# Head norm of the layer 0 memory queries: from a stage of its own into the tiles of the output gate's projection

## The reference, cut to what matters

```python
def rmsnorm(x, g):
    y = xf * lax.rsqrt(jnp.mean(xf * xf, axis=-1, keepdims=True) + EPS)
    return (y * g)

# mem_attn(pm, mkv, g_q)
q = rmsnorm(pm.reshape(b, s, MEM_HEADS, HEAD_DIM), g_q)
sc = einsum('bshd,bmhd->bhsm', q, mkv[:, :, 0]) * HEAD_DIM ** -0.5
p = softmax(sc)
o = einsum('bhsm,bmhd->bshd', p, mkv[:, :, 1])

# mlstm_mixer: o is the output gate's projection, h the normed mLSTM output
return sigmoid(o) * h
# run_trunk
x = x + concatenate([mix, mem_o]) @ w_out[l]
```

## Time and profile before

| what | value |
|---|---|
| median of 3 runs | 3421.77 us (3414.11 to 3422.32) |
| the profiled execution's own time | 3419.85 us |
| its span, first to last instruction | 3418.1 us |
| mean granted TensorE clock | 0.937 of 2.4 GHz |
| PE, DVE, ACT busy | 91%, 37%, 29% of the span |

### The profile page before, as it was taken

How to read it: one execution, slowest core, us unless ns; L and a number is a source line. 1 busy time by engine, 2 the same in 40 slices (tenths; PEclk the granted TensorE clock), 3 DMA queues, 4 the chain that set the end, 5 groups by cost and what they waited for, 6 DMA issues and landing times.

```text
span 3418.1 us, 49546 instructions
## 1 busy us (share of the span) xinstructions
PE 3093.7 (91%) x20055; PEld 2893.8 (85%) x20055; DVE 1262.7 (37%) x1969; ACT 980.7 (29%) x1658; POOL 344.3 (10%) x342
## 2 busy tenths in 40 slices
PE   6997958899999999998789689888689999999998
PEld 5997928799999999997679467777369999999998
DVE  5112751533322323341031477776143332332331
ACT  4212412423211111130431666655032321111110
POOL 0000130001000101000000234443000010000010
PEclk9998969899999999998799789999789999999999
DMA  4110042011111111112210000000411111111113
GB/s 149 58 44 13 1 131 73 32 37 47 45 50 43 47 47 48 40 52 77 90 59 29 3 1 1 2 1 23 127 75 44 43 43 50 44 48 50 45 43 123
DMA packets 63143, 169.11 MB, mean 49 GB/s; under 512 B 7334, under 2 KB 27923, under 8 KB 61859
## 3 DMA queue, kind: packets, MB, share of 16 engines
q1 hardware_dynamic: 50204, 151.00, 13.6%
q10 hardware_dynamic: 12776, 15.85, 1.4%
HBM read 153.02 MB, written 17.99 MB: 50 GB/s over the span
## 4 chain that ended last, share of the span: by engine, by line
PE 69%; DVE 6%; issue 4%; ACT 3%; DVEq 2%; SPq 2%; DMA 1%; POOL 0%; POOLq 0%; ACTq 0%
PE ps L347 57%; PE ps L2297 1%; PE ps L2254 1%; PE ps L2241 1%; PE ps L1789 1%; PE ps L1382 1%; PE ps L2243 1%; PE ps L1146 1%; PE ps L508 1%; SPq L1761 1%; SPq L1760 1%; DVE jf L2408 0%; PE ps L1349 0%; DVEq L2163 0%; PE ps L1375 0%
## 5 line engine op out<-in xcount | busy, mean ns | idle before, releaser
L347 PE MATMUL ps<-h_hi,w_hi 128*128 128x344 f32 x3360 | 725.0, 325 | 50.0 <-DVE h_lo L406 11.8
L347 PE MATMUL ps<-h_lo,w_hi 128*128 128x344 f32 x3360 | 718.5, 322 | 0.0
L347 PE MATMUL ps<-h_hi,w_lo 128*128 128x344 f32 x3360 | 714.9, 321 | 0.0
L347 PEld LDWEIGHTS ps<-h_hi,w_hi 128*128 128x128 f32 x3360 | 572.4, 190 | 56.0 <-issue 44.2
L347 PEld LDWEIGHTS ps<-h_lo,w_hi 128*128 128x128 f32 x3360 | 574.5, 191 | 0.0
L347 PEld LDWEIGHTS ps<-h_hi,w_lo 128*128 128x128 f32 x3360 | 565.1, 189 | 0.0
L299 DVE TENSOR_TENSOR w_lo<-w_raw,w_hi 128x1024 fp32r<-128x1024 f32 (+1 forms) x202 | 303.4, 1502 | 296.9 <-ACT w_hi L293 296.8
L293 ACT ACTIVATE w_hi<-w_raw 128x1024 fp32r<-128x1024 f32 (+1 forms) x202 | 208.6, 1034 | 520.5 <-PE ps L347 454.3
L1582 POOL TENSOR_TENSOR f_silu<-f_silu,nb_r 128x1032 f32<-128x1032 f32 x44 | 107.3, 2439 | 1758.1 <-ACT f_silu L1546 1758.1
L1504 DVE TENSOR_TENSOR xT<-xT,ps 128x1032 f32 (+1 forms) x64 | 78.7, 1229 | 448.3 <-PE ps L347 448.3
L347 PE MATMUL ps<-hid_hi,w_hi 128*128 128x344 f32 x1056 | 224.0, 320 | 0.0
(11 more groups left out here) (494 smaller groups left out, 3720.6 us busy)
## 6 DMA issues: line engine op xcount, KB each, us to landing
w_raw<-w_gu SPq DMA_DIRECT2D x88, 512.0 KB, 3.5
w_raw<-w_dn SPq DMA_DIRECT2D x32, 448.0 KB, 3.3
w_raw<-w_a SPq DMA_DIRECT2D x27, 512.0 KB, 3.5
w_raw<-w_o SPq DMA_DIRECT2D x16, 512.0 KB, 3.5
w_raw<-w_dn SPq DMA_DIRECT2D x16, 512.0 KB, 3.5
pages<-cmp SPq DMA_DIRECT2D x64, 128.0 KB, 2.5
w_raw<-w_b SPq DMA_DIRECT2D x9, 512.0 KB, 3.5
xT<-xT SPq DMA_DIRECT2D x1, 4128.0 KB, 17.0
```

The lines of the kernel that those rows point to most:

```text
L347: mm = pe.matmul(ps[:, 3 * slot + c, 0:cut], w[:, slot, k * P:(k + 1) * P], a[:, k, c * cut:(c + 1) * cut], start=(k == 0 and w is w_hi an ...
```

## The change

In the segment `a_o` each of the three engines gets a hook. After tile 0 ACT squares both query tiles. After tiles 1 to 4 PE does the six sum matmuls in banks 6 and 7 (two, one, two, one), and ACT takes the Ln of them; after tile 4 ACT also does both Exps, and DVE both multiplications. The stage between fence 6 and fence 7 goes, with its fence, and the later fences are renumbered (18 becomes 17). The order of the other work, SP's included, stays.

```diff
-            seg_act(act, "a_o", evac, first=True, chain=False)
+            seg_act(act, "a_o", evac, first=True, chain=False, hook=lambda i: hq_act(act, i))
...
-            seg_dve(dve, "a_o", evac, first=True, chain=False)
+            seg_dve(dve, "a_o", evac, first=True, chain=False, hook=lambda i: hq_dve(dve, i))
+        hq_p, hq_l = sem("hq_p"), sem("hq_l")
+        def hq_cuts(t, part):
+            lo, hi = ((0, 2), (2, 3))[part]
+            return hq_rt[:, t, lo * CH:hi * CH].rearrange("p (c t) -> p c t", c=hi - lo), ps[:, 6:6 + hi - lo, 0:CH]
+        def hq_act(act, i):
+            b = hn_base["act"]
+            if i == 0:
+                for t in range(2):
+                    act.activation(hq_sq[:, t, :], mix[:, 6 + t, :], ACT.Square).then_inc(hn_sq, 1)
+            elif i < 5:
+                act.wait_ge(hq_p, i)
+                out, sums = hq_cuts((i - 1) // 2, (i - 1) % 2)
+                act.activation(out, sums, ACT.Ln, bias=eps_c[:, 0:1], scale=1.0 / HD).then_inc(hq_l, 1)
+            if i == 4:
+                act.drain()
+                for t in range(2):
+                    act.activation(hq_rt[:, t, :], hq_rt[:, t, :], ACT.Exp, scale=-0.5).then_inc(hn_rt, 1)
+                hn_base["act"] += 2
+        def hq_pe(pe, i):
+            if not 1 <= i < 5:
+                return
+            t, part = (i - 1) // 2, (i - 1) % 2
+            pe.wait_ge(hn_sq, hn_base["pe"] + t + 1)
+            if i > 1:
+                pe.wait_ge(hq_l, i - 1)
+            for c in ((0, 1), (2,))[part]:
+                mm = pe.matmul(ps[:, 6 + c % 2, 0:CH], C("pairs"), hq_sq[:, t, c * CH:(c + 1) * CH], start=True,
+                               stop=True)
+            mm.then_inc(hq_p, 1)
+            if part == 1:
+                pe.sem_inc(hn_ss, 1)
...
+        def hq_dve(dve, i):
+            if i == 4:
+                hnorm_dve(dve, lambda t: mix[:, 6 + t, :], lambda t: mix[:, 6 + t, :], 2, N,
+                          lambda t: G("g_mem_q", 0), hq_rt)
...
             ogate_act(act)
             fence(act, 6)
-            hnorm_act(act, lambda t: mix[:, 6 + t, :], 2, CH, 3, hq_sq, hq_rt)
+            attend_act(act, 0)
             fence(act, 7)
-            attend_act(act, 0)
-            fence(act, 8)
...
-            seg_pe(pe, "a_o")
+            seg_pe(pe, "a_o", hook=lambda i: hq_pe(pe, i))
             fence(pe, 6)
-            hnorm_pe(pe, 2, CH, 3, hq_sq)
+            attend_pe(pe, 0)
             fence(pe, 7)
-            attend_pe(pe, 0)
-            fence(pe, 8)
```

More of the change, by code:

```diff
@@ L2464, in nsa_pool @@
             pool.memset(ckB[64:80, :, :].bitcast(F32), 0.0)
-            pool.wait_ge(fence_s, 3 * 14)
+            pool.wait_ge(fence_s, 3 * 13)
             Q_pool(pool, 0, 0)
@@ L2779, in _ @@
             load_seg(sp, "kv")
-            sp.wait_ge(fence_s, 3 * 9)
+            sp.wait_ge(fence_s, 3 * 8)
             bias_sp(sp)
@@ L2783, in _ @@
             load_seg(sp, "b_q")
-            sp.wait_ge(fence_s, 3 * 13)
+            sp.wait_ge(fence_s, 3 * 12)
             sp.dma_start(c2[:, :], A["con2"]).then_inc(con_in, 16)
             sp.dma_start(pt2[:, :], A["pt"]).then_inc(y_ld, 16)
+            sp.wait_ge(fence_s, 3 * 14)
+            snsa_sp(sp)
             sp.wait_ge(fence_s, 3 * 15)
-            snsa_sp(sp)
-            sp.wait_ge(fence_s, 3 * 16)
             mem_load(sp, 1)
@@ L2796, in _ @@
             sp.dma_start(O["o_win"], A["win"].rearrange("b r c -> b (r c)")).then_inc(sw_o, 16)
-            sp.wait_ge(fence_s, 3 * 18)
+            sp.wait_ge(fence_s, 3 * 17)
             sp.dma_start(O["o_y"], xT[:, :, :]).then_inc(sw_o, 16)
@@ L2823, in _ @@
             seg_act(act, "kv", None, chain=False)
+            fence(act, 8)
+            bias_act(act)
             fence(act, 9)
-            bias_act(act)
+            keys_act(act)
             fence(act, 10)
-            keys_act(act)
+            cmp_act(act)
             fence(act, 11)
-            cmp_act(act)
+            projb_act(act)
             fence(act, 12)
-            projb_act(act)
-            fence(act, 13)
             gates1_act(act)
             hnorm_act(act, lambda t: mix[:, t, :], 8, CH, 3, hb_sq, hb_rt)
-            fence(act, 14)
+            fence(act, 13)
             act.wait_ge(con_in, 48)
@@ L2839, in _ @@
             act.activation(gt2[:, :], gt[0:NB, NT, :], ACT.Copy)
+            fence(act, 14)
+            snsa_act(act)
             fence(act, 15)
-            snsa_act(act)
+            attend_act(act, 1)
             fence(act, 16)
-            attend_act(act, 1)
-            fence(act, 17)
             split_hi(act, segs["out1"][0], segs["out1"][0] % 2, KC)
@@ L2848, in _ @@
             ffn_act(act, 1)
-            fence(act, 18)
+            fence(act, 17)
         @block.gpsimd
@@ L2873, in _ @@
             fence(dve, 6)
-            hnorm_dve(dve, lambda t: mix[:, 6 + t, :], lambda t: mix[:, 6 + t, :], 2, N, lambda t: G("g_mem_q", 0), hq_rt)
+            attend_dve(dve, 0)
             fence(dve, 7)
-            attend_dve(dve, 0)
-            fence(dve, 8)
             split_lo(dve, segs["out0"][0], segs["out0"][0] % 2, KC)
@@ L2882, in _ @@
             kvproj_dve(dve)
+            fence(dve, 8)
+            bias_dve(dve)
             fence(dve, 9)
-            bias_dve(dve)
+            keys_dve(dve)
             fence(dve, 10)
-            keys_dve(dve)
+            cmp_dve(dve)
             fence(dve, 11)
-            cmp_dve(dve)
-            fence(dve, 12)
             projb_dve(dve)
             dve.tensor_scalar(G("g_q"), G("g_q"), 0.125, None, ALU.mult)
-            fence(dve, 13)
+            fence(dve, 12)
             hnorm_dve(dve, lambda t: mix[:, t, :], lambda t: mix[:, t, :], 8, N,
                       lambda t: G("g_q") if t < 6 else G("g_mem_q", 1), hb_rt)
-            fence(dve, 14)
+            fence(dve, 13)
             dve.wait_ge(con_in, 48)
             nsa_dve(dve)
+            fence(dve, 14)
+            snsa_dve(dve)
             fence(dve, 15)
-            snsa_dve(dve)
+            attend_dve(dve, 1)
             fence(dve, 16)
-            attend_dve(dve, 1)
-            fence(dve, 17)
             split_lo(dve, segs["out1"][0], segs["out1"][0] % 2, KC)
@@ L2906, in _ @@
             ffn_dve(dve, 1)
-            fence(dve, 18)
+            fence(dve, 17)
         @block.tensor
@@ L2930, in _ @@
             seg_pe(pe, "kv", ready=normed(2), norm=2)
+            fence(pe, 8)
+            bias_pe(pe)
             fence(pe, 9)
-            bias_pe(pe)
+            keys_pe(pe)
             fence(pe, 10)
-            keys_pe(pe)
+            cmp_pe(pe)
             fence(pe, 11)
-            cmp_pe(pe)
+            seg_pe(pe, "b_q", ready=normed(3))
             fence(pe, 12)
-            seg_pe(pe, "b_q", ready=normed(3))
-            fence(pe, 13)
             gates1_pe(pe)
             hnorm_pe(pe, 8, CH, 3, hb_sq)
-            fence(pe, 14)
+            fence(pe, 13)
             pe.wait_ge(con_in, 48)
             nsa_pe(pe)
+            fence(pe, 14)
+            snsa_pe(pe)
             fence(pe, 15)
-            snsa_pe(pe)
+            attend_pe(pe, 1)
             fence(pe, 16)
-            attend_pe(pe, 1)
-            fence(pe, 17)
             seg_pe(pe, "out1", ready=lambda k: (s_lo, 16 + k + 1))
             ffn_pe(pe, 1)
-            fence(pe, 18)
+            fence(pe, 17)
 _G = {}
```

2 lines of the change are left out of this document (added).

## The result

The changed kernel took 3406.88 us (median of 6 runs, 3400.36 to 3413.59); the kernel before, run again beside it, 3415.10 us (6 runs with the three shown above, 3412.68 to 3422.32). The ratio is 0.9969, interval 0.9956 to 0.9983: 0.31% faster, or 10.6 us, with 5.8 to 15 us in the interval; the two medians alone differ by 8.2 us. The forecast gain was 7.7 us; the forecast time, 3414.1 us, was 7.2 us too long, and the measured one lies just under the range's lower end of 3407.

A forecast was written before the change was run, and what follows sets the result against it. PE bounds the gate tiles; the 13.60 us behind them lie wholly on the path. 13.60 - 3.50 - 2.42 - 1.28 = 6.40, plus 1.30 for the clock, gives 7.7 us: 3421.77 - 7.7 = 3414.1 us, range 3407 to about 3421.

The forecast's parts named there:

- The stage of 13.60 us goes: From the last gate tile's end to the attention's first score matmul: the whole 13.60 us is removed from the path.
- A load on the path behind PE, 1.28 us: On ACT at the last gate tile: its Sigmoid needs a table load, exposed after PE has finished, costing 1.28 us.
- A second load, taken at nothing: Ahead of the attention's first Exp: a table load hidden under scores and DVE's first maximum, cost nothing; other bound 1.28 us.
- rival A: A cold start of the attention or a second exposed load takes 1.3 us: 6.4 us gained, 3415.4 us; chance 0.10.
- Rival B: The load on the path stalls ACT beyond its own row, at most 1.28 us more: 3415.4 us; chance 0.03.
- Full clock in the attention, 1.30 us: First scores start at full clock and layer 0 takes layer 1's 41.21 us to the sample part: 1.30 us gained.
- Behind the attention nothing, bound 3.3 us: Sample part and output projection of layer 0: no change taken; upper bound 3.3 us gained if they go as in layer 1.
- rival C: The clock falls at a kinder moment, sample part and `out0` going as in layer 1: 11.0 us gained, 3410.8; chance 0.27.
- Covered work, SP, the loop: ACT and DVE work under the gate tiles, SP's later loads and writing out tiles 0 to 3 all cost nothing.
- The level: The gain of 7.7 us was subtracted from 3421.77 us, the runs' median, 1.92 us above the profiled execution.
- Rival D: The clock falls in the new pause and stays at half in the attention: 12.4 us slower, 3434.2 us; chance 0.03.
- E: The attention was waiting for `mk_s` and `mv_s` anyway, so the change does nothing: 3421.8 us; chance 0.02.

The follow-up runs named there:

- e4: The changed kernel with each group of sum matmuls between the gate tiles done twice; ratio 0.9983 to the kernel before.
- e2: The kernel before with the six gate tiles written out by empty hooks, head norm still its own stage; ratio 0.9988 to the kernel before.
- e3: The changed kernel with a one-column Exp added on ACT between fence 6 and the attention; ratio 0.9963 to the kernel before.
- e12: The changed kernel with the early one-column Exp, timed a second time; ratio 0.9966 to the kernel before.
- e6: The kernel before with eight more float32 matmuls into a free bank ahead of fence 7; ratio 0.9998 to the kernel before.
- e10: The kernel before with the gate tiles written out by empty hooks, timed a second time; ratio 1.0003 to the kernel before.
- e1: The changed kernel, unaltered, timed again in more rounds; ratio 0.9978 to the kernel before.
- e5: The kernel before, unaltered, run once for a second profile; 3423.93 us.

## Why the prediction was right or wrong

The forecast time was too long because of its level: the prediction carried its gain over to 3421.77 us, the median of three runs, and that step is the one that put the time outside the range (9 below). The size of the gain came out right: 7.7 us forecast, 7.5 measured over three comparisons, and 8.6 in the stages (mean sum of the four profiles of before and written out, 144.25, less that of the three of changed, 135.64). But that was in good part luck: two steps on the table loads were wrong and others mis-sized, in opposite directions. Step by step, as the prediction put it:

1. *The stage of 13.60 us goes.* Right, and mis-sized: with the clock falling in the pause behind the gate or soon after it, two of the four profiles had 15.3 and 16.3 us. Mean 14.7. The prediction read one profile and took its clock for the rule; 1.1 us too little.
2. *Sums, 3.50 us.* Right: 3.48, shown again by e4. The segment grew by 3.6 on the mean.
3. *Emptying the last tile, 2.42 us.* Right: 2.43 in all three profiles.
4. *A load on the path behind PE, 1.28 us.* Wrong. The rule read out of rows 4, two waits: load behind PE, was the wrong rule. What decides is which wait stands ahead of the load, and a wait inside the hardware loop is not like one outside; shown by e2, where writing out the loop alone put the load ahead of the wait for PE, and by the compiled lists. The load for the last Sigmoid cost nothing: 2.43 us to the first score instead of 3.70.
5. *A second load, taken at nothing.* Wrong: with the fence's there are two waits there and not one, and `ma_m` stands ahead of the load. This is the second half of rival A, which had a chance of 0.10. The first Exp came 4.43 us after the first score; without the load it is 3.08 (e3). The bound of 1.28 us was too low: between profiles that start at full clock the exposed load is worth 2.5 us to the sample part. Steps 4 and 5 only seem to cancel: 1.3 us gained, 2.5 lost. Rival B, and with it the drain of "What ACT_TABLE_LOAD costs" in the Trainium skill, "ScalarE: Activation LUTs", gets nothing from these runs: the load at 576.23 follows the end of its Exps within 0.1 us, and from the load at 587.39 to the Exp at 588.69 are 1.30 us.
6. *Full clock in the attention, 1.30 us.* Not gained: 43.48 us to the sample part on the mean of three, against 42.18 on the mean of the four of before. Two of the three changed profiles did start at full clock, and had 43.8 and 43.7 us, over the 43 us that the prediction itself named as a sign of being wrong. The length of 41.21 us did come out, 41.1 and 41.2 us, where the second load was off the path as well (e3, e12), so what took the gain away there was step 5. But the reason given, that the start's clock decides, was not right either: e6 started at full clock and needed 43.1 us, and layer 1 needs 41.3 us also with its first scores at half clock (e6, e10). Rival A's cold start came too, in e1, and cost nothing that its length to the sample part shows.
7. *Behind the attention nothing, bound 3.3 us.* On the mean 1.3 us shorter (16.0 against 17.3), and the first profile of the changed kernel looks like rival C (sample part 10.97 us, 15.6 to the output projection). e5 and e10 show nearly the same in kernels without the change, 16.3 and 16.6 us. So scatter can account for it; that the change favours the short form is not excluded with so few profiles.
8. *Covered work, SP, the loop.* Right: no idle time of PE inside the segment, transfers landed in time, writing out worth nothing.
9. *The level.* This is what put the time outside. The gain was taken from the median of three runs, 3421.77, after adding 1.92 us to the profiled execution. The kernel before, in four groups of 6 to 35 runs, has medians of 3415.1, 3416.9, 3417.9 and 3416.5 us, and single runs from 3406.6 to 3428.7. Three runs were 5 us too high, and the allowance of 4 us for scatter was too small for two medians of few runs. With 3416.9 the same gain gives 3409.2, as the later medians of 3408.6 and 3411.5 bear out; the first one, 3406.88, was itself a low draw. Of the miss of 7.2 us the level is about 5 us by that figure, and 6.7 us by the median of 3415.10 measured beside the changed kernel.

Rival D, slower through a clock that stays at half, was not seen in any of the profiles. E, a change without effect, is ruled out: PE waited for neither `mk_s` nor `mv_s`, and all three intervals lie below 1.

## What to carry to other kernels

A stage removed between barriers gives what stood on the path in it, and work moved under a busy TensorE costs its TensorE part: here 3.5 us paid for 12.3 removed. When a move mixes activation functions, look in the compiled instructions at which wait stands ahead of the table load, and put a one-column activation where the engine is idle anyway: one line brought the first Exp 1.35 us forward and the sample part 2.3 us. Before a forecast to a few us, get the level and its scatter from more than three runs, and a stage's length from more than one profile, since the clock alone moved the same stage between 13.6 and 16.3 us.

## What was not expected of the hardware

The same pause of 3.62 us of PE behind the gate left the clock at 1.00 in two profiles (before, e2); in three others it fell in the pause (e6, e10) or soon behind it (e5), and the sums took 6.40, 6.37 and 5.40 us instead of 3.72. Starting the attention at full clock didn't by itself shorten it: 41.1 to 43.8 us to the sample part with such a start, 41.8 to 43.0 without. An exposed table load of 1.28 us came with 2.5 us more to the sample part; the half clock behind it lasted 6.8 instead of 3.4 us. And 16 added matmuls of 128 columns among 64 of 4 columns didn't keep the clock at 1.00; they took their own time, much of it at half clock.
